# Even mixer of a two-layer encoder: order of the input projections, place of the pooled projection, and the engine that sums its windows

## What is computed

```python
def multiscale_pool(p, pool_w, pool_scale):
    # 4 groups of 128 channels, windows 2, 4, 8, 16: mean over positions
    # t-w/2 .. t+w/2-1 (clipped at the borders), minus the token itself,
    # then a 128x128 matrix of the group
    ...
def even_mixer(h, w_in, conv_w, conv_b, ln_g, ln_b, pool_w, pool_scale, w_out):
    z = h @ w_in                                                    # (B, S, 1536)
    a, gate, p = z[..., :D_A], z[..., D_A:2 * D_A], z[..., 2 * D_A:]
    ya = conformer_conv(a, gate, conv_w, conv_b, ln_g, ln_b)   # a*sigmoid(gate), 31-wide depthwise conv, layernorm, silu
    yb = multiscale_pool(p, pool_w, pool_scale)
    return jnp.concatenate([ya, yb], axis=-1) @ w_out
```

## Time and profile before

| what | value |
|---|---|
| time, median of 3 runs | 2596.23 us (2594.76 to 2598.92) |
| time of the profiled execution | 2597.54 us |
| its span, slowest core (core 1) | 2596.1 us |
| spans of the 8 cores | 2591.2 to 2596.1 us |
| granted PE clock, mean | 0.992 |
| busy: PE, DVE, ACT, POOL | 98%, 32%, 24%, 16% |

### The profile page before, as it was taken

The page is one execution under the profiler, slowest core; times in us unless marked ns, Lnnn a source line. Parts: engine busy times, 40 slices in busy tenths (PEclk is TensorE's granted clock), DMA queues, the critical chain, the costliest instruction groups (busy, mean ns, idle before and its releaser), DMA issues.

```text
span 2596.1 us, 38890 instructions; the slowest of 8 cores (2591.2 to 2596.1 us)
## 1 busy us (share of the span) xinstructions
PE 2542.7 (98%) x12955; PEld 1205.2 (46%) x12955; DVE 837.4 (32%) x1280; ACT 628.6 (24%) x1094; POOL 404.3 (16%) x701
## 2 busy tenths in 40 slices
PE   6999899999999999999999999999999999999998
PEld 3447444444444444444444474444444444444443
DVE  3425543223222222212224674232222222222212
ACT  3434543132111111111133363211111111211111
POOL 1200232101110111011023531210111011101100
PEclk8999999999999999999999999999999999999999
DMA  8986599856763896456461467994476457634522
GB/s 175 230 168 127 139 150 186 145 159 123 132 132 133 137 165 138 134 78 89 127 140 35 109 121 156 163 160 112 106 132 121 117 118 126 126 108 100 80 43 98
DMA packets 318541, 333.52 MB, mean 128 GB/s; under 512 B 146432, under 2 KB 276368, under 8 KB 318224
## 3 DMA queue, kind: packets, MB, share of 16 engines
q0 software_dynamic: 122096, 118.40, 33.7%
q1 hardware_dynamic: 186608, 203.72, 28.2%
q10 hardware_dynamic: 9648, 8.92, 1.1%
HBM read 331.92 MB, written 83.89 MB: 160 GB/s over the span
## 4 chain that ended last, share of the span: by engine, by line
PE 95%; DMA 3%; issue 1%; DVE 1%; ACT 0%; POOL 0%; SPq 0%; DVEq 0%; ACTq 0%; POOLq 0%
PE ps L171 95%; DMA pdr<-pst 1%; DMA w_in<-ev_w_in 1%; DMA xin<-x 0%; DMA xr<-x 0%; DMA xres<-xr 0%; DMA BIG<-hb 0%; DVE vt L1178 0%; DVE bst L855 0%; DVE xr L484 0%; DVE A L424 0%; ACT pst L422 0%; DVE bst L1163 0%; ACT BIG L902 0%; POOL rs L373 0%
## 5 line engine op out<-in xcount | busy, mean ns | idle before, releaser
L171 PE MATMUL ps<-BIG,wgu 128*128 128x512 bf16 x5632 | 1226.0, 379 | 0.0
L171 PEld LDWEIGHTS ps<-BIG,wgu 128*128 128x128 bf16 x5632 | 550.5, 98 | 662.6 <-issue 0.3
L171 PE MATMUL ps<-wd,gT 128*128 128x512 bf16 x2816 | 609.1, 379 | 0.0
L510 DVE TENSOR_TENSOR gT<-tmp,ps 128x512 bf16<-128x512 f32 x352 | 241.8, 687 | 842.2 <-PE ps L171 814.5
L171 PEld LDWEIGHTS ps<-wd,gT 128*128 128x128 bf16 x2816 | 275.6, 98 | 332.2
L508 ACT ACTIVATE tmp<-ps 128x512 f32<-128x512 f32 x352 | 209.2, 594 | 777.0 <-PE ps L171 733.3
L171 PE MATMUL ps<-w_in,BIG 128*128 128x512 bf16 (+1 forms) x1344 | 289.7, 373 | 6.3 <-ACT pst L422 4.3
L185 POOL DMA_DIRECT2D wgu<-ffn_wgu x176 | 134.1, 762 | 852.6 <-PE ps L171 823.7
L171 PE MATMUL ps<-w_out,BIG 128*128 128x512 bf16 x1024 | 233.9, 382 | 3.6 <-ACT BIG L902 1.5
L387 ACT ACTIVATE hb<-xr 128x1024 bf16<-128x1024 f32 x80 | 84.5, 1057 | 552.7 <-DVE xr L533 275.0
L171 PEld LDWEIGHTS ps<-w_in,BIG 128*128 128x128 bf16 x1344 | 131.9, 99 | 151.2 <-issue 11.1
(11 more groups left out here) (130 smaller groups left out, 1110.3 us busy)
## 6 DMA issues: line engine op xcount, KB each, us to landing
wgu<-ffn_wgu POOLq DMA_DIRECT2D x176, 512.0 KB, 6.5
xr<-xr SPq DMA_DIRECT2D x59, 512.0 KB, 4.0
xin<-x SPq DMA_DIRECT2D x32, 512.0 KB, 6.2
xr<-xres SPq DMA_DIRECT2D x32, 512.0 KB, 4.7
xnat<-xr SPq DMA_DIRECT2D x32, 512.0 KB, 3.4
out<-xr SPq DMA_DIRECT2D x31, 512.0 KB, 2.9
xr<-x SPq DMA_DIRECT2D x28, 512.0 KB, 5.9
xres<-xr SPq DMA_DIRECT2D x28, 512.0 KB, 4.1
```

Source lines behind the costliest of these rows:

```text
L171: ins = self.nc.tensor.matmul(o, lhsT=l, rhs=r, start=st, stop=sp)
L510: k.op(dve, lambda e: e.tensor_tensor(out=gT[:, j, tg * 512:(tg + 1) * 512], in0=tmp[:], in1=ps[:, bl[1], :], op=ALU.mult), reads=[d_tmp, ...
```

## The change

* The order of the weights and of the work at the start: WG and WA first halves first, then `ag_half(t, 0)` for tiles 0 to 3, then the second halves, then `ag`; WP comes last. The issue of the later weights stands in POOL's queue behind the statistics of tile 2 (WG, WA second halves) and of tile 4 (WP). `n_load` waits for WA's first half (tiles 2, 3), WG's second (4, 5), WA's second (6, 7), WP (8 on). The norm's weight row is loaded as one row and spread to 128 partitions by two PE matmuls instead of a 512 KB DMA and a DVE multiply. `tr_pe` is evicted by ACT. Transposes are issued 2 tiles ahead of use.
* `p_proj` becomes `pq(tq)`, channels on the partitions: for four tiles at once 4 banks of 8 matmuls of 512 columns, evicted by ACT straight into four blocks of `BIG` of those tiles (blocks 0 to 3 for tiles 0 to 15, 4 to 7 for the others). `pq(0)` stands behind `ag(5)`, `pq(1)` to `pq(5)` behind `ag(7)`, `ag(11)` ... `ag(23)`, `pq(6)` behind the last `ag`, and `pq(7)` in `feed0(-2)`, among the first layernorm steps (its four evictions on DVE). `pdr`, `p_load`, `band` and `pool_bank` go.
* `pool_units` makes the window sums on DVE by doubling: in slices of 64 columns, for each group one `first` (two adds from `BIG` into f32 scratch), 0 to 3 `level`s (two adds each, f32) and one `final` (two `scalar_tensor_tensor`: sum / w minus the token, into `BIG` blocks 4 to 7), with a few instructions of up to 8 elements for borders: 28 units for tiles 0 to 15, two of them behind each `ag(t)` from t = 17 to 30, and 28 for tiles 16 to 31, in FFN pass 0: one behind each of j = 5 to 9, then up to four behind each j from 10 until they are done.
* The scratch of the first 28 lies at 158 KB, of the others at 108 KB. So `w_out` has to wait for the scratch, `wd` rows 0 to 5 are loaded at j = 17 to 19 instead of 0 to 5, and the residual ring of the prologue starts with its three `xr` buffers, the two `xp` buffers being added behind `pq(7)`.

The core of the diff:

```diff
-        for i, hs in ((WP, (0, 1)), (WG, (0,)), (WA, (0,)), (WG, (1,)), (WA, (1,))):
...
+        w_load(WG, (0,))
+        w_load(WA, (0,))
...
+            gate = [] if t < 2 else [d_w[WA][0]] if t < 4 else [d_w[WG][1]] if t < 6 else [d_w[WA][1]] if t < 8 else d_w[WP]
...
-        k.mm([(ps[:, b, :], warm[:, 0:128], warm[:], True, True) for _ in range(26)], reads=[d_warm], writes=[psd[b]])
+        k.mm([(ps[:, b, :], warm[:, 0:128], warm[:], True, True) for _ in range(20)], reads=[d_warm], writes=[psd[b]])
+        k.mm([(ps[:, 6 + h, :], ones32[0:1, :], grow[0:1, h * 512:(h + 1) * 512], True, True) for h in range(2)],
...
-            evac(0, pst[:, r, :], ps[:, b, :], [psd[b]], [d_pst[r]])
-            k.dma(act, [(by_phase(pdr)[t // 16, t % 16], pst[:, r, :])], reads=[d_pst[r]], addw=[d_pdr[t // 16]],
-                  own=d_pst[r])
+        def pq_mm(tq, g):
+            b = k.banks(1)
+            ts = range(4 * tq, 4 * tq + 4)
+            k.mm([(ps[:, b, :], w_in[:, WP, kk, g * 128:(g + 1) * 128], BIG[:, 4 * tq:4 * tq + 4, kk, :], kk == 0,
+                   kk == 7) for kk in range(8)], reads=d_w[WP] + [x for t in ts for x in dB[t]], writes=[psd[b]])
+            return b
+
+        def pq_out(tq, g, b, eng=0):
+            hi = tq // 4
+            evac(eng, BIG[:, 4 * tq:4 * tq + 4, 4 * hi + g, :], ps[:, b, :].rearrange("p (t q) -> p t q", t=4),
+                 [psd[b]], addw=[dB[t][hi] for t in range(4 * tq, 4 * tq + 4)])
...
+                        def level(cur=cur, nxt=nxt, sh=sh):
+                            (a, da), (b_, db) = cur, nxt
+                            tt(b_[:, 0:16 - sh, :], a[:, 0:16 - sh, :], a[:, sh:16, :], ALU.add, [da], writes=[db])
+                            tt(b_[:, 16 - sh:16, 0:65], a[:, 16 - sh:16, 0:65], a[:, 0:sh, 1:66], ALU.add, [da],
+                               addw=[db])
...
+                        def fin(o0, o1, s_ap):
+                            k.op(dve, lambda e: e.scalar_tensor_tensor(
+                                out=out_(o0, o1, q0, q0 + 64), in0=s_ap, scalar=1.0 / w, in1=X(o0, o1, g, q0, q0 + 64),
+                                op0=ALU.mult, op1=ALU.subtract), reads=[dS] + dX(o0, o1), addw=wr(o0, o1))
...
+            if t % 4 == 3 and 7 <= t < 24:
+                pq(t // 4)
...
+            if t >= 17:
+                for fn in units[:2]:
+                    fn()
+                units = units[2:]
+        for i in range(8):
+            u_tr(1, i)
+        for fn in units:
+            fn()
+        pq(6)
...
-        for tg in range(8):
-            for g in range(4):
-                pool_bank(tg, g)
...
+                bs = [pq_mm(7, g) for g in range(3)]
+                ln_silu(0)
+                bs.append(pq_mm(7, 3))
+                for g in range(4):
+                    pq_out(7, g, bs[g], 1)
...
+            if 5 <= j < 17:
+                for _ in range(1 if j < 10 else 4):
+                    if pu:
+                        pu.pop(0)()
...
-        wd_at = {j: [j] for j in range(6)}
+        wd_at = {17 + n: [2 * n, 2 * n + 1] for n in range(3)}
```

More of the change, by code:

```diff
@@ L232, in make_consts @@
     wins = (2, 4, 8, 16)
-    band = np.zeros((4, 5, 128, 128), dtype=np.float64)
+    edge = np.zeros((4, 2, 8))
     for g, w in enumerate(wins):
         half = w // 2
[L236 to L249, removed]
+        for o in range(half):
+            edge[g, 0, o] = 1.0 / (o + half)
+        for n, o in enumerate(range(17 - half, 16)):
+            edge[g, 1, n] = 1.0 / (16 - o + half)
+    c["pedge"] = np.ascontiguousarray(np.broadcast_to(edge.reshape(1, 4, 2, 8), (128, 4, 2, 8))).astype(np.float32)
     c["ident"] = np.eye(128, dtype=np.float32)
@@ L740, in u_tr @@
                   reads=[d_U[hf]], addw=[d_UT[i][hf]], transpose=True)
[L742 to L786, removed]
+        def tt(o, a, b_, op, reads, writes=(), addw=()):
+            k.op(dve, lambda e: e.tensor_tensor(out=o, in0=a, in1=b_, op=op), reads=reads, writes=writes, addw=addw)
@@ new lines, in tr_in @@
+        def tr_in(t):
+            nrm.scale(t)
+            nrm.tr_pe(t, ident, d_ident, 0)
+        head((0, 1))
+        tr_in(0)
+        tr_in(1)
+        ag_half(0, 0)
+        ag_half(1, 0)
+        head((2, 3))
+        n_load(4)
+        n_load(5)
+        tr_in(2)
+        tr_in(3)
+        ag_half(2, 0)
+        ag_half(3, 0)
+        head((4, 5))
+        for t in (6, 7, 8, 9):
+            n_load(t)
+        for t in range(3):
+            ag_half(t, 1)
+        tr_in(4)
+        ag_half(3, 1)
@@ L798, in norm_step @@
                 n_stat(i)
-        for fn, t in jobs:
-            if fn == p_proj:
-                while ni[0] < min(t + 5 if t < 6 else t + 8, NT + 3):
-                    norm_step()
[L804 to L807, removed]
-                u_tr(0, t - 16)
-            if fn == ag and t == 25:
-                p_load(0, 15, 132 * KB)
+        units = []
+        for t in range(4, NT):
+            if t == 5:
+                head((6,))
+            if t == 6:
+                tr_in(7)
+            if t >= 6:
+                while ni[0] < min(11 if t == 6 else t + 6, NT + 3):
+                    norm_step()
+            ag(t)
+            if t == 5:
+                tr_in(6)
+                head((7,))
+                pq(0)
+            late_consts(t)
+            if 16 <= t < 24:
+                u_tr(0, t - 16)
+            if t % 4 == 3 and 7 <= t < 24:
+                pq(t // 4)
+            if t == 16:
+                bufs, ed, d_ed, su, d_su = ptmp(158 * KB)
+                units = pool_units(0, bufs, ed, d_ed, su, d_su, lambda sl, g: 0 if sl == 0 else None)
+                for g in range(4):
+                    k.op(dve, lambda e: e.tensor_copy(out=hx[:, g, :], in_=BIG[:, 8:16, g, 127]),
+                         reads=[dB[o][0] for o in range(8, 16)], addw=[d_hx])
+            if t >= 17:
[7 more added lines that the diff above has]
+        pq(6)
         W0, d_W0 = k.buf("Wc", 96 * KB, [4, 48, 8], BF16)
@@ L950, in build @@
         xr = Ring(slots)
-        xpro = Ring([(xpt[:, i], d_xpt[i]) for i in range(2)] + slots)
+        xpro = Ring(list(slots))
         hbp = ring("hbp", 96 * KB, [D], BF16, 4)
```

156 lines of the change are left out of this document (123 added, 33 removed).

## The result

The changed kernel takes 2608.47 us (median of seven executions), against 2597.57 for the kernel before (six executions, in the same rounds; 2596.23 in the three runs shown first). The ratio is 1.0041, 95% interval [1.0025, 1.0057]: **0.41% slower**, where 2586.5, faster, was forecast. The profiled execution took 2607.81 us, 10.3 more than the one of before.

What follows compares the result with a forecast made beforehand. PE, busy 98% of the span, was taken as the bound. Terms of -23.0, -6.9, -5, +1.9, +19, +1.5, +1 and +2 sum to -9.5 us, giving 2586.5 us; eight-in-ten range 2570 to 2603.

Steps and rivals of the forecast that it cites:

- the start: Input stage: reordered weight loads put PE ahead, gapless from about 52 us; -5 us, between +3 and -9.
- its transposes: Input stage: transposes issued 2 tiles ahead instead of 4 land slightly late; +1 us (0 to 3).
- the clock after the hold: Convs: PE's clock falls while it waits, half of the prologue's 3; +1.5 us (0 to 3).
- the units in the FFN: FFN pass 0: DVE window sums of tiles 16 to 31 slightly exceed PE's time; +2 us (0 to 5).
- the prologue: Before the FFN: pq(7)'s four DVE evictions delay layernorm statistics and first residual add; +1.9 us (0 to 3).
- the hold: Before conv 3: DVE units, then eight transposes sharing DMA engines with w_out, keep PE waiting; +19 us (9 to 26).
- the end: From the first down matmul to the end of the span: forecast change 0.
- Band matmuls: Between projections and convs: 23.0 us of PE work all goes; -23.0 us.
- pq(7) in the hole: Its 32 matmuls leave the input stage for PE's idle, slow-clock time at the layernorm; -6.9 us.
- The unit: One DVE window-sum step, some 1050 elements in two instructions, costs 1.5 us.
- the slower rival: DVE becomes the bound in FFN pass 0 and from tile 24; at 2.1 us per unit, 2609 us; chance 0.11.
- the hold and the start eat it all: Longer wait before conv 3 and smaller start gain leave the result within 0.2% (5.2 us); chance 0.20.

Runs made afterwards that it cites:

- Experiment 2: Changed kernel with 24 unread 512-column matmuls ahead of conv 0 and 24 behind conv 2: 0.9991 of the kernel before, profiled execution 2593.3 us.
- experiment 11: Changed kernel with w_out after the transposes, 18 unread matmuls, spread FFN units, earlier scales of tiles 4 to 7, rotated wd sum: 0.9919 of the kernel before, median 2575.03 us.
- experiment 12: The kernel of experiment 11 without its 18 unread matmuls behind conv 2: 0.9952 of the kernel before, profiled execution 2584.66 us.
- experiment 5: Kernel before, without its 376 band matmuls and their evictions, all else as it was: 1.0041 of the kernel before.
- experiment 4: Changed kernel with all w_in loads issued at the start, not behind the statistics of tiles 2 and 4: 1.0049 of the kernel before.
- experiment 7: Changed kernel with the norm's scale of tiles 4 to 7 issued on DVE ahead of the products: 1.0004 of the kernel before.
- experiment 3: Changed kernel without the 28 DVE units of tiles 16 to 31 in FFN pass 0: 1.0018 of the kernel before, median 2598.6 us.
- experiment 1: Changed kernel with w_out's four pieces waiting for the last transpose of U: 0.998 of the kernel before, profiled execution 2590.03 us.

## Why the prediction was wrong, point by point

The time left the range on the slow side. By the means of the table the misses are: the start and its transposes 5.4 us more than forecast, the clock after the hold 5.8, the units in the FFN 6.2, the prologue 1.2; the hold was 3.1 less and the end 1.5 less. The spread between the cores, which has no term at all, adds 5.9.

**Band matmuls, -23.0, and pq(7) in the hole, -6.9: right as PE work.** No `band` group is left; what they covered is in the hold and in the clock below. The last gate or value matmul came 12.4 sooner; 13.8 of it is pq(6) and pq(7) out of the way. In 262 to 285 the clock is 1.00; a fall like that of the earlier trace rows is left on five cores, 3 to 4 us long (292 to 296 on core 7; twice on core 6). The prologue took 3.1 more instead of 1.9.

**The hold, +19: right in mechanism and nearly in size.** `w_out` and the transposes met (24.3 us against 23 reckoned). The 16.5 that it took for the transposes of before is a little short: the eighth landed at 226.76, 17.0 after the first issue. DVE was less late than thought: the last product came some 3.6 after the last `ag`'s matmuls, not 8. From the last gate or value matmul to conv 3 PE needs 13.8 for pq(6) and three convs and took 28.9 (29.7 in the mean): 15 to 16 lost.

**The unit, 1.5: right,** if a little high (four instructions of two units take 2.75), and with it the slower rival falls. DVE forms in 150 to 202 (busy us, mean ns):

```profile
L739 DVE TENSOR_TENSOR psum_w<-BIG 128x975 f32<-128x975 bf16 x5 | 5.8, 1170 | 0.1
...
L739 DVE TENSOR_TENSOR psum_w<-psum_w 128x528 f32<-128x528 f32 x2 | 1.4, 702 | 0.0
L739 DVE TENSOR_TENSOR psum_w<-psum_w 128x520 f32<-128x520 f32 x2 | 1.4, 695 | 0.0
...
L813 DVE SCALAR_TENSOR_TENSOR BIG<-psum_w,BIG 128x512 bf16<-128x512 f32 x4 | 2.6, 687 | 0.1
```

The 528 and the 520 are the two adds of one `level`. The 520 f32 elements with one source that starts at an odd column take 695, the 528 with both at an even one 702: 1.34 ns an element and 1.33, fixed part included. The price is that of the earlier trace rows (688 for 512: 1.34). The rule of the Trainium skill that the prediction weighed (Vector Engine (DVE) Microarchitecture Reference, Measured stream behaviour on trn2) gives 1.30 against 1.05 ns an element where both sources start on an odd word; here one of the two does, and the trace shows no difference. No run here has both odd.

**Clock after the hold, +1.5 (0 to 3): this step failed.** It measured +7.3 in the mean and +13.4 on the slowest core. It was taken as half of the prologue's 3, "the clock falling while PE waits anyway": that the clock is down for the wait and little longer. It isn't so here. On core 7 it is at 0.50 until 35 us behind the end of the wait. Experiment 2 raises the clock without touching the wait and takes 14 us off; experiments 11 and 12 differ in that alone, by 13 us in the profiled executions; experiment 5 makes the same fall in the kernel before. The term had a second mistake, that it is a mean: the time at the low clock differs between cores, and the metric takes the worst of eight (the 5.9 of spread).

**Start, -5 (+3 to -9): wrong by 5.4, with its transposes' +1.** It was reckoned from when the weights land, and they land as reckoned (second halves at 32.3 and 36.2, WP at 49.8 on core 7, against 30, 35 and near 50). But PE was to be gapless from 52, and it isn't: it hardly waits for weights (experiment 4). What it waits for is the order on DVE, in the timeline of PE in the changed kernel (core 7; tiles 4, 5 and 6):

```profile
44.61 1.01 PE L171 MATMUL ps<-ident,hb 128*128 128x128 bf16 x8 [3.74 <-DVE hb L379]
...
51.22 1.01 PE L171 MATMUL ps<-ident,hb 128*128 128x128 bf16 x8 [2.19 <-DVE hb L379]
...
63.74 1.01 PE L171 MATMUL ps<-ident,hb 128*128 128x128 bf16 x8 [2.24 <-DVE hb L379]
```

The scale of each of these tiles stands behind the product of a tile before, whose sigmoid waits for PE; so PE waits for DVE three times (the expectation of experiment 7 counts four; tile 7, behind `pq(0)`, has no such wait), and the clock is at 1.2 GHz for 17 of the 24 us from 43 to 67 (on the other cores less). Experiment 7 moves the scales and ends the stage 3.5 us ahead of the forecast. Windows of 50 to 75, changed kernel (core 7) and experiment 7 (core 5), each the slowest core:

```profile
50.00:75.00 25.00, 21.15 (x94) 9.85 (x95) 4.61 (x5) 7.32 (x13) 1.48 (x4) 0.79 0.26 85
```

```profile
50.00:75.00 25.00, 24.61 (x127) 11.57 (x126) 9.72 (x10) 13.17 (x24) 5.13 (x14) 1.00 0.43 136
```

**Units in the FFN, +2 (0 to 5): +8.2.** PE's waits in 320 to 512 of the changed kernel:

```profile
PE ps L171 <- DVE gT L496: 3.6, 3, 1.8
PE ps L171 <- ACT vn L984: 2.2, 2, 1.5
...
PE ps L171 <- ACT tmp L494: 0.4, 1, 0.4
```

The waits on `gT` and `tmp` are those forecast and within the bound. Missed were those on `vn`: a unit at j = 5 to 9 stands ahead of the layernorm pieces on DVE, and PE's transposes of `vn` wait; without the units (experiment 3) no such wait is in the stage. Behind the second of them 32 matmuls take 8.75 instead of 7.07, the clock falling again:

```profile
403.54 0.38 PE L171 MATMUL ps<-ident,vn 128*128 128x128 bf16 x4 [1.51 <-ACT vn L984]
...
404.51 8.75 PE L171 MATMUL ps<-BIG,wgu 128*128 128x512 bf16 x32
```

The waits, 6.2 us, and this 1.7 are nearly all of the loss. The later `wd` rows, put at nothing, cost nothing on seven cores; on core 4 PE waits for them at 499.6 and 502.7 (1.6 and 2.7 us), the clock falls, and from the first down matmul to the end it takes 2102.4 instead of 2095.4 to 2096.6.

Of the rivals, "the hold and the start eat it all" was nearest in its places, and none had the clock as a price of its own. The rival that ends slower has the measured time, 2609, in it; that is luck. It gets there by a unit of 2.1 us, and the units took 1.4. Where DVE did hold PE up, in the start and in the FFN, it was by the order of its instructions.

## What to carry to other kernels

Work that is taken off the bounding engine may have been the cover of something: before counting its time as won, list what ran under it, and give the engine's clock a line of its own where a gap of a few us opens ahead of small matmuls (2.8 to 7.3 us here). Where the metric is the slowest of several cores, a loss that differs from core to core and from run to run costs its worst case and not its mean. A transfer that a freed buffer sets off (`w_out`) is best tied to the end of the transfers that the critical path waits for: one dependency was worth 0.6% here.

## What the runs showed of the hardware that was not expected

* After a gap of 4.4 to 7.3 us (of 2.8 to 4.1 in experiment 1) the clock can stay at 1.2 GHz through conv work in which PE is busy 90 to 100%. In the changed kernel it came back at 225 on core 6, after 7 us, and at 262 on core 7, after 51, the last 35 of them without an idle stretch; the cores run the same instructions. The Trainium skill (TensorE: Matmul & The Clock Gate, What's actually happening) has the full clock return once the engine is active again; core 6 agrees with that, core 7 doesn't (0.50 and 0.51 from 225 to 262). The conv matmuls have 128 columns and a weight load each; in the FFN, behind matmuls of 512 columns, the clock came back after 3 to 4 us on the six cores where it fell near 400. That the shape is the cause wasn't tried, and why the time differs so between cores stays open.
* Eight DMA transposes take 12.5 to 13.8 us without `w_out` beside them and 23.9 to 26.9 beside its four loads with conversion to bf16.

Not tried: another place for `z0`, so that conv 3 would not wait at all, and an earlier buffer for `wd` rows 0 to 5, whose wait (3 to 4 us in experiment 11) is the largest that is left.
